# GpSimd takes a quarter of the weights' low halves, and the mixing of modulation weights moves between engines, in a two-layer trunk kernel

## The reference

```python
cond = silu(c)
for l in range(2):
    mod = cond @ w_ada[l] + b_ada[l]                 # 2048 x 12288
    sh1, sc1, g1, sh2, sc2, g2 = split(mod, 6)
    h = rms_norm(x) * (1 + sc1) + sh1
    z = h @ w_in[l]                                  # 2048 x 4160
    # three head groups on columns of z: differential attention (6 heads), latent attention
    # with w_uq, w_ukv and a rotary key (6 heads), spatial gating
    mix = concatenate([out_a, out_b, out_c]) @ w_out[l]      # 2048 x 2048
    x = x + g1 * mix
    h = rms_norm(x) * (1 + sc2) + sh2
    a = h @ w_up[l]                                  # 2048 x 11264
    y = conv_b + causal convolution of a with 3 taps
    g, val = split(y, 2)
    x = x + g2 * ((silu(g) * val) @ w_down[l])       # 5632 x 2048
```

## Time and profile before

| | |
|---|---|
| median of 3 runs | 2528.46 us (2524.81 to 2529.74) |
| the profiled execution | 2523.4 us, its span 2521.6 us |
| TensorE busy | 2422.4 us (96%) |
| VectorE busy | 1796.8 us (71%) |
| ScalarE busy | 1122.5 us (45%) |
| GpSimd busy | 536.5 us (21%) |
| mean granted TensorE clock | 0.975 |

### The profile page before, as it was taken

One profiled execution on the slowest core, in us unless ns is written; L12 is line 12 of the kernel. 1 busy time (PEld: TensorE's weight loads), 2 busy tenths in 40 slices (PEclk: granted clock), 3 DMA queues, 4 the chain that ended last, 5 costly groups with the idle time before them and its releaser, 6 DMA issues.

```text
span 2521.6 us, 37553 instructions
## 1 busy us (share of the span) xinstructions
PE 2422.4 (96%) x15080; PEld 2025.7 (80%) x15080; DVE 1796.8 (71%) x2477; ACT 1122.5 (45%) x1549; POOL 536.5 (21%) x565
## 2 busy tenths in 40 slices
PE   6799999989999999999999999999999999999999
PEld 2578778768888888888878888777888888888888
DVE  2455657987668889989986477788766566665765
ACT  2233555345443454445444355534544344443543
POOL 3332310132322133213330120002231002200220
PEclk8899999999999999999999999999999999999999
DMA  9999886677779888898787677556776556555654
GB/s 311 340 300 313 263 265 205 207 244 242 252 257 316 277 257 266 295 297 253 255 267 230 202 234 219 180 170 210 243 247 213 185 187 188 184 187 188 185 185 149
DMA packets 450509, 596.86 MB, mean 237 GB/s; under 512 B 24172, under 2 KB 397984, under 8 KB 450080
## 3 DMA queue, kind: packets, MB, share of 16 engines
q1 hardware_dynamic: 394640, 392.47, 49.1%
q0 software_dynamic: 55296, 201.35, 24.4%
q10 hardware_dynamic: 400, 0.65, 0.1%
HBM read 592.30 MB, written 2.10 MB: 236 GB/s over the span
## 4 chain that ended last, share of the span: by engine, by line
PE 85%; DVE 6%; DMA 3%; issue 3%; ACT 2%; POOL 0%; ACTq 0%; DVEq 0%; SPq 0%; POOLq 0%
PE bank L1029 85%; DMA ada<-in_w_ada_dram 3%; DVE wlo L1594 1%; ACT whi L1351 1%; DVE acc L1588 1%; DVE xT L1632 1%; DMA rows<-in_b_ada_dram 0%; DVE r L1651 0%; DVE T L1666 0%; DVE hx L1687 0%; ACT hx L1418 0%; PE bank L1320 0%; DMA raw<-in_w_in_dram 0%; ACT sq L1404 0%; DVE xT L1633 0%
## 5 line engine op out<-in xcount | busy, mean ns | idle before, releaser
L1029 PE MATMUL bank<-hx,whi 128*128 128x512 f32 (+1 forms) x3968 | 1365.6, 391 | 4.1 <-DVE hx L1689 4.1
L1594 DVE TENSOR_TENSOR wlo<-raw,whi 128x1024 fp32r<-128x1024 f32 (+1 forms) x774 | 936.6, 1216 | 593.9 <-ACT whi L1351 592.6
L1351 ACT ACTIVATE whi<-raw 128x1024 fp32r<-128x1024 f32 (+1 forms) x774 | 785.3, 1019 | 1118.2 <-PE bank L1029 1093.7
L1029 PE MATMUL bank<-hx,wlo 128*128 128x256 f32 x3840 | 1096.5, 286 | 31.2 <-DVE hx L1687 10.8
L1029 PEld LDWEIGHTS bank<-hx,whi 128*128 128x128 f32 x3968 | 744.7, 190 | 165.6 <-DVE hx L1689 4.8
L1029 PEld LDWEIGHTS bank<-hx,wlo 128*128 128x128 f32 x3840 | 733.5, 191 | 62.7 <-issue 25.1
L1029 PE MATMUL bank<-mx,whi 128*128 128x512 f32 x1728 | 618.5, 400 | 0.0
L1029 PE MATMUL bank<-mx,wlo 128*128 128x256 f32 x1728 | 495.5, 287 | 2.7 <-DVE wlo L1594 1.2
L983 POOL DMA_DIRECT2D ada<-in_w_ada_dram x384 | 253.9, 664 | 1135.5 <-DVE acc L1588 581.9
L1029 PEld LDWEIGHTS bank<-mx,whi 128*128 128x128 f32 x1728 | 329.6, 191 | 76.1
L1029 PEld LDWEIGHTS bank<-mx,wlo 128*128 128x128 f32 x1728 | 331.6, 192 | 15.4 <-issue 10.6
(11 more groups left out here) (163 smaller groups left out, 1326.6 us busy)
## 6 DMA issues: line engine op xcount, KB each, us to landing
ada<-in_w_ada_dram POOLq DMA_DIRECT2D x384, 512.0 KB, 6.3
raw<-in_ffn_w_up_dram SPq DMA_DIRECT2D x352, 512.0 KB, 4.5
raw<-in_ffn_w_down_dram SPq DMA_DIRECT2D x176, 512.0 KB, 4.0
raw<-in_w_in_dram SPq DMA_DIRECT2D x128, 512.0 KB, 5.4
raw<-in_w_out_dram SPq DMA_DIRECT2D x48, 512.0 KB, 4.8
raw<-in_w_out_dram SPq DMA_DIRECT2D x32, 256.0 KB, 3.1
raw<-in_mla_w_uq_dram SPq DMA_DIRECT2D x12, 384.0 KB, 4.2
raw<-in_mla_w_ukv_dram SPq DMA_DIRECT2D x6, 512.0 KB, 4.9
```

What stands on the lines that cost most here:

```text
L1029: return pe.matmul(out_, lhsT, rhs, start=start, stop=stop, skip_group_check=True)
L1351: return act.activation(out_, in_, ACT.Copy)
L1594: i_ = tt(dst, src, high.bitcast(F32), ALU.subtract)
```

## The change

1. **Low halves.** For the 704 units of 1024 words (without `w_ukv`), VectorE makes columns 0 to 767 of `wlo` and GpSimd columns 768 to 1023, both after `hi_ready`. GpSimd counts `lo_pool`; TensorE and SyncE wait for both counts (`wait_low`).
2. **Modulation.** `VECTOR_BATCHES` (5 batches, 10 halves) becomes `VECTOR_HALVES`, 13 of 24 halves: 4, 10 to 19, 22 and 23. So the first half of batch 2 and batches 5 to 9 and 11 go over VectorE; before, it was batches 4, 6, 7, 8 and 10. The spreading (`ada_over`) changes in the projections. Batches 5, 9 and 11 are the next ones at the three transitions, so none of them has a burst now.
3. **Three matmuls.** The pairs 9 to 13 of the input projection, all of the output projection and the last column pair of the third down pass use `three`. Their banks are emptied by one ScalarE copy (`win`) or one `xT` update (`wout`, last down pair).
4. **Order.** `av` steps, and `prob` steps whose `exp` does not stand in the same stretch, go between `hi` and `lo`. Some steps of the projections are grouped anew.

```diff
+LAST_DOWN = (len(PASS_BLOCKS) - 1, 7)
...
+TWO_PAIRS = DAQ_PAIRS + DAK_PAIRS
...
+SPREAD_FROM = (SGV_PAIRS[0], QA_PAIRS[1])
...
-VECTOR_BATCHES = (4, 6, 7, 8, 10)
+VECTOR_HALVES = (4, 10, 11, 12, 13, 14, 15, 16, 17, 18, 19, 22, 23)
...
-        return self.ada_g // 8 in VECTOR_BATCHES
+        return self.ada_g // 4 in VECTOR_HALVES
...
-        if l == 0:
-            self.ada_over(5, 18 + 30 + 22)
-        else:
-            self.ada_over(11, 28 + 30 + 24 + 12)
+        self.ada_over(3 if l == 0 else 10, 36)
...
+            if pair == SPREAD_FROM[l]:
+
+                self.ada_over(5 if l == 0 else 11, 4 * len(LATE_PAIRS[LATE_PAIRS.index(pair):]) - 2 + 24 + 10)
...
         self.drain()
+        self.add("ms", l, j, 0)
+
+        spare = not self.vector_next()
+        if spare:
+            self.burst()
+        self.add("ms", l, j, 14)
+        self.add("ms", l, j, 15)
         self.add("root", l, j)
         self.add("inv", l, j)
-        if not self.vector_next():
-
+        if spare:
             self.burst()
...
             while split < min(limit or used + SPLITS, len(self.units)):
                 steps.append(("hi", split))
+                steps.extend(ready)
+                ready = []
                 steps.append(("lo", split))
                 split += 1
...
+            ready = [x for x in own if x[0] == "av" or (x[0] == "prob" and ("exp", *x[1:]) not in own)]
+            splits(None, ready)
...
+        def shared(u):
+
+            return words(u) == UNIT and units[u].what != "ukv"
+
+        pool_count = list(itertools.accumulate(int(shared(u)) for u in range(len(units))))
+
+        def wait_low(eng, u):
+
+            eng.wait_ge(lo_ready, u + 1)
+            if pool_count[u]:
+                eng.wait_ge(lo_pool, pool_count[u])
...
-                    sp.wait_ge(lo_ready, u - RAWS + 1)
+                    wait_low(sp, u - RAWS)
...
+                elif t[0] == "lo":
+                    u = t[1]
+                    if shared(u):
+                        pool.wait_ge(hi_ready, u + 1)
+                        ((src, dst),), ((_, high),) = split_views(u, wlo), split_views(u, whi)
+                        pool.tensor_tensor(dst[:, 3 * S:UNIT], src[:, 3 * S:UNIT], high[:, 3 * S:UNIT].bitcast(F32),
+                                           ALU.subtract).then_inc(lo_pool, 1)
...
-                    pe.wait_ge(lo_ready, u + 1)
+                    wait_low(pe, u)
...
+                            elif x_.what == "win" and x_.i not in TWO_PAIRS:
+                                i_ = three(b[:, 0:S], wh, wl, hi(hx, k), lo(hx, k), start, stop)
                             elif x_.what == "wout":
-                                i_ = paired(b, wh, wl, mixed(k), start, stop)
+                                i_ = three(b[:, 0:S], wh, wl, mixed(k)[:, 0:S], mixed(k)[:, S:2 * S], start, stop)
+                            elif x_.what == "down" and (x_.b, x_.i) == LAST_DOWN:
+                                i_ = three(b[:, 0:S], wh, wl, hi(mx, k), lo(mx, k), start, stop)
...
                     for (src, dst), (_, high) in zip(split_views(u, wlo), split_views(u, whi)):
+                        if shared(u):
+                            src, dst, high = (a[:, 0:3 * S] for a in (src, dst, high))
                         i_ = tt(dst, src, high.bitcast(F32), ALU.subtract)
...
-                    order.after(stt(xa, b[:, S:2 * S], g, xa, ALU.mult, ALU.add))
+                        if (ph, pair) != LAST_DOWN:
+                            order.after(stt(xa, b[:, S:2 * S], g, xa, ALU.mult, ALU.add))
                     stt(xa, b[:, 0:S], g, xa, ALU.mult, ALU.add).then_inc(emptied_dve, 1)
```

More of the change, by code:

```diff
@@ L391, in out_projection @@
         self.ada_flush_for(6 * l + 3)
+        for kind in ("T", "H", "L"):
+            for k in range(2):
+                self.add(kind, l, "kva", k)
         self.steps.extend([("sg", l, 0), ("sg", l, 1), ("Tsg", l, 0), ("Tsg", l, 1)])
@@ L582, in empties @@
         if k in ("copy", "addz"):
-            return ("act" if k == "copy" and t[2] in TOKEN_PAIRS else "dve"), [("win", *t[1:])]
+            return ("act" if k == "copy" and t[2] not in TWO_PAIRS else "dve"), [("win", *t[1:])]
         if k == "res":
@@ L1363, in _ @@
                     i_.then_inc(hi_ready, 1)
-                elif kind == "copy" and t[2] in TOKEN_PAIRS:
+                elif kind == "copy" and t[2] not in TWO_PAIRS:
                     l, pair, c_, ph = t[1:]
```

66 lines of the change are left out of this document (38 added, 28 removed).

## The result

The changed kernel takes 2560.6 us (median of 4, 2557.4 to 2561.9), the kernel before 2529.1 beside it: a ratio of 1.0125, 95% interval 1.0108 to 1.0143. It is slower by 32 us, where 14 less were forecast, and lies 9 us outside the range of 2482 to 2552.

A forecast was written before the change was run, and what follows sets the result against it. TensorE, busy 96% of the span, was taken as the bound. Bursts -15, three matmuls +12, output projections -32 and shared low halves +21 summed to -14: 2509 us profiled, 2514 median, range 2482 to 2552.

The forecast's parts named there:

- The low half on two engines: +21: 704 shared units: VectorE and GpSimd block each other, costing +21 us, with ends 0 and +59.
- 0.14 us of overlap: At each handover between VectorE and GpSimd, both were said to progress together for 0.14 us.
- +59: Upper end of the loss from splitting low halves between VectorE and GpSimd.
- the bound was 41: First up passes: sharing low halves was said to lose between 0 and 41 us.
- the sum at exactly the beat: First up passes: two-source work of VectorE and GpSimd summed to 2.77 us a unit, equal to TensorE's 2.77.
- The queue behind a gate: GpSimd's next quarter finishes 4.9 to 5.8 us after a gate starts, against 5.5 us of look-ahead.
- what I put at nothing: Loads behind quarters, SyncE reloads, TensorE's extra wait, regrouped steps and moved `acc` and `prob` were said to cost nothing.
- Output projections: -32: Both layers' output projections: relieving VectorE regains TensorE idle time and clock, -32 us: about 20 in layer 0, 12 in layer 1.
- the lower end of 10: Smallest output-projection gain, -10 us, if chains stay; the other end was -66.
- Bursts, -15: TensorE: twelve fewer modulation bursts, nine of them gaining, give -15 us, between -13 and -21.
- three matmuls, +12: 880 k-blocks in input, output and down projections use three matmuls, 0.014 us more each: +12 us.
- The slower one: Rival: VectorE and GpSimd's shared way becomes the bound; 2534 to 2568 us, chance 0.30.

The follow-up runs named there:

- the fills: Changed kernel, GpSimd filling its 256 columns with zeros, reading no SBUF: one fill 2480.2 us, ratio 0.981; eight fills of 32 columns 2484.9 us, 0.983.
- no sharing: Changed kernel with VectorE making all 1024 columns of every low half again, the rest of the change kept: 2509.5 us, ratio 0.992.
- the one run on it: Changed kernel with VectorE making all 1024 columns, and `paired` instead of `three` in the first sweep of both output projections: 2508.2 us, ratio 0.992.
- run with 16 halves: Changed kernel with VectorE making all 1024 columns, 16 half-batches, and layer 0's output-sweep `acc` placed as before the change (22 and 9): 2503.1 us, ratio 0.990.
- both runs with ten: Changed kernel with the earlier ten half-batches on VectorE: with GpSimd's quarter 2579.5 us, ratio 1.020; with VectorE making all columns 2541.6 us, 1.005.
- the run with 128 columns: Changed kernel with 128 of the 1024 low-half columns on GpSimd instead of 256, and 896 on VectorE: 2541.8 us, ratio 1.004.

## Why the prediction was wrong

Two terms fell by their sizes, and some costs that the sum had at nothing were there.

*The low half on two engines: +21.* The single costs held: 0.95 and 0.72 us alone, 1.50 with the other's turn, 1.57 for the pair where 1.5 was said. That the two block each other while both have two SBUF operands is borne out by the fills: without the reads 80 us come back, 75 with a longer queue. The rule of the Trainium skill (SBUF — State Buffer, "Who interferes with whom") pointed the right way. The pair's 1.57 us is 0.10 less than the 1.67 of the two alone, so most of the 0.14 us of overlap that I gave a handover is there. Whether both engines read in it is open: operations of VectorE alone overlap by 0.08 in the records too (the one at 511.66 for 1.22 us and the next at 512.80). The step that failed is the choice of +21 between 0 and +59, with the reason that a nearly full queue alone costs little. Against the fills, the first up passes lost 17.6 and 16.9 us (35 where the bound was 41), layer 0's later ones 7.8 and 6.0 (14 of 18). So with the sum at exactly the beat the loss was near the upper end: a sum of means that is equal to the deadline leaves nothing for the places where a gate, an `acc` and two low halves meet, and the order has such places in every pass. The queue behind a gate was worked out at 4.9 to 5.8 us against 5.5 of look-ahead; the row above shows 7.0, as the gate's own products are stretched as well. And what I put at nothing was not: 8 us in layer 0's down passes, 10 in the input projections, 3 in the output projections, and 10 in layer 1 by the beat described below. These make up the 78 us between the two profiled executions. Put as the forecast's sum, with no sharing as the base: sharing cost 51 us where +21 was said, and all the rest gave 19 where 35 was said. These two make the 46 us between -14 and +32.

*Output projections: -32.* TensorE had 33 us more to do in them (14 more bursts at 1.86 us, 512 k-blocks at 0.014), and the four sweeps went from 359.0 to 378.6: the relief is 14 us, near the lower end of 10. It came where the prediction had looked, in the second sweeps, but was less than half of what was said. Layer 0's went from 57.5 to 51.5 with two more bursts in it, 11 us of relief: TensorE's four waits there for low halves (6.2 us, the row below) are gone, and the sweep's clock rose from 0.94 to 0.99. Layer 1's went from 50.4 to 47.8, 4 us. The first sweeps gave nothing. VectorE was relieved in them too, but TensorE's longest wait in layer 0's first sweep (2.7 us) was for the rotary part's `mqr` and none was for a low half, and the bursts that took the place of 22 `acc` cost their full price: 122.8 to 142.2, where eight bursts and the three matmuls make 17 of the 19 us. The step that failed is that idle time and lost clock of a whole stage were put down to the engine that was busiest in it. The clock of the first sweep is 0.94 before and after. Who TensorE waited for in layer 0's second sweep of the kernel before (us in sum, times, longest), and then layer 0's rotary part, in the first sweep, before and after:

```profile
PE bank L1029 <- DVE wlo L1594: 6.2, 4, 2.5
```

```profile
421.00:451.00 30.00, 27.26 (x126) 21.64 (x126) 25.27 (x44) 7.61 (x13) 2.64 (x5) 0.83 0.63 191
```

```profile
420.00:450.00 30.00, 26.52 (x160) 21.92 (x161) 15.44 (x35) 4.97 (x8) 6.75 (x7) 0.77 0.59 193
```

VectorE's busy time falls from 25.3 to 15.4 us of 30, and the granted clock does not rise. Its fall from 0.83 to 0.77 says little, as the figure depends on where the 30 us are taken (415 to 445 us of the kernel before give 0.89). In both kernels TensorE waits for `mqr` (2.74 and 2.15 us), makes short matmuls, and starts the next weight matmuls at the lower of its two levels, 0.64 us a k-block where it takes 0.36 at the higher; that the chain brings the lower clock was not tested.

*Bursts, -15, and three matmuls, +12.* The bursts are 1408 records, as said. Where they left the first up passes, these took 11.4 and 10.4 us less for seven each (196.9 to 185.5 and 195.7 to 185.3, with the fills), 1.6 a burst. But with all low halves on VectorE they took only 4.6 and 3.6 less: the 32 `acc` that came in their place fill VectorE to 183 of 192 us, and TensorE is idle for 5.7 us in layer 0's. So some 14 of the bursts' us went to the `acc` even without GpSimd, a price that the sum had at nothing. Whether `three` costs 12 us was not settled: the one run on it shows 1.3 us where 5 were expected. Left out of the sum was a small gain: the input projections became 12.7 and 8.0 us shorter; eleven bursts less are 20 of these, `three` takes back 4, and some 5 remain that no term named.

*The rivals.* The slower one is what happened, in its mechanism and in its amount: 2560.6 in its 2534 to 2568. It had 0.30, and its upper end held +59 for the low halves and half of the relief, both near what came. The test that I gave for it, over 205 us in the first up pass (194 before), was set too high: by that cut the passes took 200.4 and 199.9. Seven bursts less would have made it 181 with nothing in the way. That TensorE would wait for GpSimd's quarter in the later up passes was named as what makes the forecast wrong, and there 10 of 11 waits are that.

The Trainium skill's warning (Perfetto Trace Analysis, "Optimizing Scalar/DVE Operations"), that work moved from VectorE to GpSimd may not help because of the shared port, is what the chip shows: VectorE's 1832 us with sharing and 1827 without.

## What to carry to other kernels

Work that reads two operands from SBUF is not taken off VectorE by giving it to GpSimd: add the two engines' such work as if it ran on one, and where the sum comes to the beat, as it did here, take the upper bound of the loss, because the gates and the large operations meet somewhere. Before a stage's idle time and lost clock are counted as gain, find the single waits in it and who ends each; a busy engine beside them is no proof. Cut stages at the same instruction in every run, and compare the beat of undisturbed stretches before a difference is put down to the change. And work that is spread up to a deadline has to be out well ahead of it, or it is flushed there in one block.

## What the runs showed of the hardware

TensorE has two steady beats for the same pair of matmuls (256 columns, then 512) at full clock. Layer 1 after 2100 us, the kernel before and then the one without sharing, 100 us each, with TensorE busy throughout in both:

```profile
2100.00:2200.00 100.00, 100.00 (x568) 86.73 (x568) 69.05 (x87) 48.84 (x58) 19.64 (x12) 1.00 0.60 187
```

```profile
2100.00:2200.00 100.00, 100.00 (x579) 88.19 (x578) 71.71 (x91) 49.76 (x59) 24.62 (x15) 1.00 0.61 190
```

568 against 579 matmuls in the same time. From one 512-column matmul's start to the next it is 347 ns in the fast beat, pair after pair, and a repeating 361, 349, 350 in the slow one, 353 in the mean. The starts of TensorE's matmuls in the kernel before:

```profile
2099.82 0.28 PE L1029 MATMUL bank<-hx,wlo 128*128 128x256 f32 x1
2099.94 0.40 PE L1029 MATMUL bank<-hx,whi 128*128 128x512 f32 x1
2100.18 0.28 PE L1029 MATMUL bank<-hx,wlo 128*128 128x256 f32 x1
2100.30 0.40 PE L1029 MATMUL bank<-hx,whi 128*128 128x512 f32 x1
2100.54 0.28 PE L1029 MATMUL bank<-hx,wlo 128*128 128x256 f32 x1
```

A beat holds as long as nothing disturbs the row, for over 500 us here, and can change at a burst or a wait: the run that shares outside the up projections goes from the fast to the slow one at a wait of 0.13 us at 2227 us. The kernel before is in the slow one from 1922 to 2463 us and the changed kernel from 1992 to 2498, so it adds nothing between these two; the kernel without sharing and both with fills are in the fast one there. That is 9.6 us between the changed kernel and the one without sharing (180.9 against 177.5, 90.6 and 90.4 against 88.7, 135.7 against 133.1 us a pass). So about 10 of the 51 us of sharing and of the 80 of the fills are the beat and not a wait, and likewise about 10 of the 19 that the kernel without sharing gains on the kernel before. The run with 16 halves is in the fast beat too, both runs with ten in the slow one. Which disturbance leaves which beat stays open, and so does whether it explains the wide spread of the run with 128 columns: of the executions that were not profiled there is no trace.
